# A two-layer decoder in one kernel: another order of heads, transposes and jobs in the top-k indexer, and a shorter selection

## The reference

```
logits = einsum('bqhd,bkd->bqhk', qi, k_idx) * (IDX_DIM ** -0.5)       # 8 heads of 64
score  = einsum('bqhk,bqh->bqk', relu(logits), wi * (IDX_HEADS ** -0.5))
score  = where(causal, score, -inf)
_, idx = top_k(score, 256)          # the 256 best keys of a query; ties go to the lower index
```

## Time and profile before

| | |
|---|---|
| median of three runs | 1347.61 us (1347.42 to 1348.81) |
| the profiled execution, its own time | 1348.37 us |
| its span (first to last instruction) | 1346.5 us |
| TensorE busy | 1302.9 us, 97% |
| VectorE busy | 803.5 us, 60% |
| ScalarE busy | 563.1 us, 42% |
| GpSimd busy | 524.6 us, 39% |
| granted TensorE clock, mean | 0.99 |

### The profile page before, as it was taken

How to read it: one execution, slowest core, us unless ns; L and a number is a source line. 1 busy time by engine, 2 the same in 40 slices (tenths; PEclk the granted TensorE clock), 3 DMA queues, 4 the chain that set the end, 5 groups by cost and what they waited for, 6 DMA issues and landing times. The chain is left out here.

```text
span 1346.5 us, 19019 instructions
## 1 busy us (share of the span) xinstructions
PE 1302.9 (97%) x6890; PEld 1111.5 (83%) x6890; DVE 803.5 (60%) x1581; ACT 563.1 (42%) x1134; POOL 524.6 (39%) x721
## 2 busy tenths in 40 slices
PE   9999999999999999999987999999899999999997
PEld 8878888989898888888766788888788988888885
DVE  7624755555556345245577889977977776345233
ACT  8312244554454023123235665564266666023122
POOL 2842034554443744234401132331066564744201
PEclk9999999999999999999998999999999999999999
DMA  6232331121101522133300122342222221521122
GB/s 203 77 106 78 112 116 56 55 71 48 55 32 56 175 87 75 60 96 120 95 0 1 55 87 89 110 140 67 88 72 64 79 63 64 153 95 59 60 65 87
DMA packets 83372, 110.07 MB, mean 82 GB/s; under 512 B 9552, under 2 KB 45648, under 8 KB 83280
## 3 DMA queue, kind: packets, MB, share of 16 engines
q1 hardware_dynamic: 83280, 108.86, 26.0%
HBM read 81.04 MB, written 27.79 MB: 81 GB/s over the span
## 5 line engine op out<-in xcount | busy, mean ns | idle before, releaser
L1700 PE MATMUL psum<-ring_hi,act_lo 128*128 128x512 f32 x816 | 322.4, 395 | 0.7 <-DVE act_lo L1688 0.7
L1702 PE MATMUL psum<-ring_hi,act_hi 128*128 128x512 f32 x816 | 318.9, 391 | 0.0
L1701 PE MATMUL psum<-ring_lo,act_hi 128*128 128x512 f32 x816 | 318.8, 391 | 0.0
L1126 POOL CAST ring_hi<-raw 128x512 fp32r<-128x512 f32 x128 | 81.8, 639 | 322.6 <-DMA raw<-in_dsa_w_in 144.0
L1341 DVE TENSOR_TENSOR act_lo<-psum,act_hi 128x512 fp32r<-128x512 f32 (+3 forms) x276 | 156.0, 594 | 67.2 <-ACT act_hi L1170 40.9
L1129 POOL TENSOR_TENSOR ring_lo<-raw,ring_hi 128x512 fp32r<-128x512 f32 x128 | 180.0, 1406 | 10.4
L1700 PEld LDWEIGHTS psum<-ring_hi,act_lo 128*128 128x128 f32 x816 | 154.1, 189 | 32.8 <-DVE act_lo L1688 1.4
L1702 PEld LDWEIGHTS psum<-ring_hi,act_hi 128*128 128x128 f32 x816 | 153.8, 188 | 32.3
L1701 PEld LDWEIGHTS psum<-ring_lo,act_hi 128*128 128x128 f32 x816 | 154.1, 189 | 31.0
L1170 ACT ACTIVATE act_hi<-psum 128x512 fp32r<-128x512 f32 (+1 forms) x244 | 114.9, 511 | 150.2 <-PE psum L1912 80.5
L1140 POOL TENSOR_TENSOR small<-small 128x1 f32<-128x1 f32 x128 | 70.7, 552 | 228.7 <-ACT p L1308 169.8
(11 more groups left out here) (257 smaller groups left out, 2473.7 us busy)
## 6 DMA issues: line engine op xcount, KB each, us to landing
raw<-in_dsa_w_in SPq DMA_DIRECT2D x48, 256.0 KB, 3.1
gz<-z_scratch SPq DMA_DIRECT2D x16, 512.0 KB, 3.6
raw<-in_ple_w_gate SPq DMA_DIRECT2D x32, 256.0 KB, 3.1
raw<-in_mla_w_in SPq DMA_DIRECT2D x19, 256.0 KB, 2.9
xr<-in_x_t SPq DMA_DIRECT2D x16, 256.0 KB, 6.8
z_scratch<-gz SPq DMA_DIRECT2D x16, 256.0 KB, 2.0
raw<-in_mla_w_out SPq DMA_DIRECT2D x16, 256.0 KB, 3.4
p<-in_x SPq DMA_DIRECT2D x16, 256.0 KB, 3.1
```

What stands on the lines that cost most here:

```text
L1126: last = nc.gpsimd.tensor_copy(dst, src[:, c0:c0 + cols])
L1700: nc.tensor.matmul(dst, lhs(1), rhs(0), start=start, stop=False)
L1701: nc.tensor.matmul(dst, lhs(0), rhs(1), start=False, stop=False)
L1702: return nc.tensor.matmul(dst, lhs(0), rhs(0), start=False, stop=stop)
```

## The change

In the indexer, heads are single steps (one bank or one pair each) instead of pairs, and all jobs from the first head on (heads, transposes, projections) take ring A and ring B in turn (`next_ring`). The order within tile t becomes: heads 0 to 3 of t, transposes of t+1, query job of t+2, heads 4 to 7. In tiles 6 and 7, which have no further query job, a key/value job stands there (`KV_EARLY = 2`), so six are left behind the indexer. The third query job is issued before the heads of tile 2. The rotated query rows go to two slots at the end of `xr` instead of `p1`, and there is a third ReLU row slot behind the scores. The weights of the key/value chunk are issued ahead of the heads, not one piece per query job.

In the search ScalarE counts tiles 5, 6, 7 (before 3, 6, 7), VectorE 2, 3, 4. There are still 32 rounds; gate jobs 2 and 5 carry two, since two key/value jobs no longer carry one. `last_step` counts only ScalarE's tiles and sets the threshold; `above` is gone. In `sel`, ScalarE makes a row of signs with its sum in `xr` behind the scores, and VectorE has an equality pass, a running count with a start value, a small step for the limit, and one last pass. The tiles are selected in the order 6, 4, 7, 3, 5, 2.

```diff
-SEARCH = [2, 4, 5, 3, 6, 7]
-ACT_TILES = [3, 6, 7]
+SEARCH = [2, 3, 4, 5, 6, 7]
+ACT_TILES = [5, 6, 7]
+KV_EARLY = 2
+TWO_ROUNDS = (2, 5)
+SELECT = [6, 4, 7, 3, 5, 2]
...
+    kv_weights(0, 1)
+    qi_job(FULL)
+    kv_weights(2, 3)
     fk.append(key_job(1, 0, 1).after["fk"])
     rots = [key_back(1, job, fk[job]).after["rot"] for job in range(2)]
-    qi_ready = {FULL: qi_split(FULL, rot[FULL])}
-    rot[FULL + 1] = qi_job(FULL + 1)
+    qi_split(FULL)
+    kv_weights(4)
+    qi_job(FULL + 1)
+    kv_weights(5)
     for job in range(2):
         lo_at["kiT"] = key_split(1, job, rots[job])
-    for t in range(FULL, T):
+    qi_job(FULL + 2)
+    kv_weights(6, 7)
+    idx_scores(FULL, range(4))
+    qi_split(FULL + 1, next_ring())
+    idx_scores(FULL, range(4, IDX_HEADS))
+    add("idx_mask", None, t=FULL)
+    for t in range(FULL + 1, T):
+        idx_scores(t, range(4))
         if t + 1 < T:
-            qi_ready[t + 1] = qi_split(t + 1, rot[t + 1])
+            qi_split(t + 1, next_ring())
         if t + 2 < T:
-            rot[t + 2] = qi_job(t + 2)
-        idx_scores(t, qi_ready[t])
+            qi_job(t + 2, next_ring())
+        elif t - T + 2 < KV_EARLY:
+            kv_job(t - T + 2, next_ring())
+        idx_scores(t, range(4, IDX_HEADS))
+        add("idx_mask", None, t=t)
...
+    for t in range(KV_EARLY, T):
+        for job in range(KV_EARLY) if t == KV_EARLY else ():
+            ahead(next_chunk(1, 2), job)
+        ahead(next_chunk(1, 2), t)
+        kv_job(t)
+        search()
...
-    after_bits = [("last_step", None, {}), ("above", None, {})]
-    after_bits += [("sel", {"found": 1}, {"t": t}) for t in range(FULL, T)]
+    after_bits = [("last_step", {"thr": 1}, {})]
+    after_bits += [("sel", {"found": 1, "sgn": 1}, {"t": t, "side_free": max(0, j - 1)}) for j, t in enumerate(SELECT)]

     def z_extra(k):
         search()
+        if k in TWO_ROUNDS:
+            search()
...
+        relu_rows = [gz[:], t2[:], xr[:, SCORE_AT[T]:SCORE_AT[T] + S]]
...
             if n > CW:
-                return (gz, t2)[k % 2][:, 0:n]
-            return (gz, t2)[k // 2 % 2][:, k % 2 * CW:k % 2 * CW + n]
+                return relu_rows[k % 3][:, 0:n]
+            return relu_rows[k // 2 % 3][:, k % 2 * CW:k % 2 * CW + n]
...
+                    k = s.before["sc"]
+                    act_e.wait_ge(sem["b_full"], s.after["b_full"])
+                    if n["keys"] > CW:
+                        act_e.wait_ge(sem["sc"], max(k - 2, 2 * IDX_HEADS))
+                    elif k >= 6:
+                        act_e.wait_ge(sem["sc"], k - 5)
+                    elif k == 0:
+                        act_e.wait_ge(sem[n["gfree"][0]], n["gfree"][1])
+                    elif k == 4:
+                        act_e.wait_ge(sem["x2_st"], n["x2"])
...
                             dve.wait_ge(sem["cs_ld"], n["cs"])
-                            dve.wait_ge(sem["hi"], s.before["hi"])
+                            dve.wait_ge(sem["x2_st"], n["x2"])
+                            if n["stack_read"]:
+                                dve.wait_ge(sem["hi"], n["stack_read"])
...
-                    for i, t in enumerate(SEARCH):
+                    linked(nc.vector.memset(cnt[:, 0:SPREAD - len(ACT_TILES)], 0.0))
+                    for t in ACT_TILES:
+                        i = SEARCH.index(t)
...
                     linked(nc.vector.tensor_scalar(eq, score_at(t), thr, None, ALU.is_equal))
-                    linked(nc.vector.tensor_tensor_scan(order, eq, eq, 0.0, ALU.add, ALU.max))
-                    linked(nc.vector.scalar_tensor_tensor(eq, order, need[:, i:i + 1], eq, ALU.is_le, ALU.mult))
-                    nc.vector.scalar_tensor_tensor(score_at(t), score_at(t), thr, eq, ALU.is_gt,
-                                                   ALU.add).then_inc(sem["found"], 1)
+                    linked(nc.vector.tensor_tensor_scan(order, eq, eq, float(2 * keys - 4 * TOPK), ALU.add, ALU.add))
+                    dve.wait_ge(sem["sgn"], s.after["sgn"])
+                    linked(nc.vector.scalar_tensor_tensor(need[:, i:i + 1], order[:, keys - 1:keys], 0.5, cnt[:, i:i + 1],
+                                                          ALU.mult, ALU.add))
+                    nc.vector.scalar_tensor_tensor(score_at(t), order, need[:, i:i + 1], side_at(t), ALU.is_le,
+                                                   ALU.is_gt).then_inc(sem["found"], 1)
```

More of the change, by code:

```diff
@@ L606, in plan @@
     last_rows = tail(0, 4, "in1", ("lo", now["lo"]))
-    def idx_scores(t, q_ready):
-        keys = (t + 1) * P
[L611 to L617, removed]
@@ L618, in plan, with next_ring, idx_scores @@
-    idx_n = [0]
+    turn = [0]
+    def next_ring():
+        turn[0] += 1
+        return "BA"[turn[0] % 2]
+    def idx_scores(t, heads):
+        keys = (t + 1) * P
+        for h in heads:
+            add("idx", {"b_full": 1, "relu": 1, "sc": 1}, ring=next_ring(), jobs=1, freed=["relu"],
+                wide=keys > CW, t=t, h=h, keys=keys, q_ready=max(qi_ready[t], lo_at["kiT"]),
+                x2=now["x2_st"], gfree=read_by["G"])
     fk = [key_job(1, 0, 0).after["fk"]]
     norm_b(last_rows[0], 0, last_rows[1])
-    def qi_job(t):
-        w(next_chunk(1, 1), t)
-        return rope_job(1, 1, t, t % 2, cs=cs.after["cs_ld"]).after["rot"]
@@ L626, in qi_split, with qi_job @@
[L626 to L631, removed]
+    rot, qi_ready, stack_read = {}, {}, {}
+    def qi_job(t, ring="A"):
+        rot[t] = rope_job(1, 1, t, t % 2, cs=cs.after["cs_ld"], stack_read=stack_read.get(t - 2), ring=ring,
+                          x2=now["x2_st"]).after["rot"]
@@ new lines, in qi_split, with kv_job, kv_weights @@
+    def qi_split(t, ring="B"):
+        s = add("qi_split", {"b_full": 2, "hi": 2, "lo": 2}, ring=ring, jobs=2, freed=["lo"], slot=t % 2, rot=rot[t])
+        stack_read[t] = s.after["hi"]
+        qi_ready[t] = s.after["lo"]
+    def kv_job(t, ring="A"):
+        slot = t % 2
+        rope_job(1, 2, t, slot, extra_inc={"st%d" % slot: 1, "vcopy": 1}, st_before=now["st%d" % slot], ring=ring)
+    def kv_weights(*rows):
+        for d in rows:
+            w(next_chunk(1, 1), d)
+    kv_weights(0, 1)
@@ L663, in search @@
         search_end(search_begin())
-    n = 0
-    for i, name in ((2, "kv"), (3, "q"), (4, "q")):
+    for t in range(KV_EARLY, T):
[4 more added lines that the diff above has]
+        search()
+    for i in (3, 4):
         for t in range(T):
             ahead(next_chunk(1, i), t)
[L669 to L679, removed]
+            slot = t % 2
+            st = search_begin()
+            rope_job(1, i, t, slot, extra_inc={"st%d" % slot: 1}, base=(i - 3) * CW, st_before=now["st%d" % slot])
+            search_end(st)
     q_stored = (now["st0"], now["st1"])
@@ L1295, in _ @@
                 elif k == "idx":
[L1296 to L1304, removed]
+                    k = s.before["sc"]
[8 more added lines that the diff above has]
+                        act_e.wait_ge(sem["x2_st"], n["x2"])
+                    nc.scalar.activation(relu_slot(k, n["keys"]), bank(s.banks[0], n["keys"]), ACT.Relu,
+                                         scale=IDX_SCALE).then_inc(sem["relu"], 1)
                 elif k == "E":
@@ L1548, in _ @@
                     dve.wait_ge(sem["widx"], s.before["widx"])
[L1549 to L1558, removed]
-                            nc.vector.tensor_scalar(dst, src, wcol, None, ALU.mult).then_inc(sem["sc"], 1)
-                        else:
-                            nc.vector.scalar_tensor_tensor(dst, src, wcol, dst, ALU.mult, ALU.add).then_inc(sem["sc"], 1)
+                    h, k = n["h"], s.before["sc"]
+                    dve.wait_ge(sem["relu"], s.after["relu"])
+                    if k == 0:
+                        dve.wait_ge(sem["x2_st"], n["x2"])
+                    else:
+                        dve.wait_ge(sem["sc"], k)
+                    src = relu_slot(k, n["keys"])
+                    wcol = wis[:, t * IDX_HEADS + h:t * IDX_HEADS + h + 1]
+                    if h == 0:
+                        nc.vector.tensor_scalar(dst, src, wcol, None, ALU.mult).then_inc(sem["sc"], 1)
+                    else:
+                        nc.vector.scalar_tensor_tensor(dst, src, wcol, dst, ALU.mult, ALU.add).then_inc(sem["sc"], 1)
                 elif k == "idx_mask":
@@ L1759, in _ @@
                             c = (4 * j + i) * P
-                            last = nc.tensor.transpose(bank(s.banks[j])[:, i * P:(i + 1) * P], p1[:, c:c + P], ident[:])
+                            last = nc.tensor.transpose(bank(s.banks[j])[:, i * P:(i + 1) * P],
+                                                       qi_stack(n["slot"])[:, c:c + P], ident[:])
                         last.then_inc(sem["b_full"], 1)
```

41 lines of the change are left out of this document (23 added, 18 removed).

## The result

The changed kernel takes **1332.75 us** (median of 4 runs, 1332.07 to 1333.47) against 1347.51 us for the kernel before on the same chip: a ratio of 0.9892, 95% interval 0.9876 to 0.9907, some 14.8 us faster. A second set, on another chip, gave 1333.64 against 1347.34 us, 0.9898 (0.9885 to 0.9912). The forecast was 1331.2 us in a range of 1325.5 to 1339.5. The profiled execution took 1332.53 us.

The account below looks back on a forecast made before the run. TensorE, busy nearly all of 1346.5 us, bounds the kernel; only the indexer and the border can give. 1348.37 less 16.4 (indexer 16.2, border 0.2) is 1332.0, less 0.76 to the median: 1331.2 us; range 1325.5 to 1339.5.

Parts of the forecast that it names:

- two common points: Indexer: from the end of the keys' transposes (665.33 us) to the end of last head and two key/value jobs.
- the large ones: Indexer: TensorE pauses of 3.4 us before tile 3's later heads and 2.4 us before tile 5's transposes.
- Low clock twice: Indexer: after each of the two large pauses TensorE runs at its low clock level, losing 1.4 us each time.
- my 67.6: Indexer: TensorE's work in us between the two points, from transposes 4.0, jobs 32.7 and heads 30.9.
- The new order, step by step: Indexer: walk through the new order of heads, transposes and jobs; last head ends at 743.2, 16.2 us off TensorE's path.
- rival (a): Indexer: only the last tiles gain, pauses of tiles 3 to 5 return; 8.8 us, 1338.8 us; chance 12%.
- Rival (d): Indexer: TensorE's clock stays low with more waits, so slower; 1388 us if from tile 3 on; chance 5%.
- this half at 0.2 us: Search and selection: the attention starts 0.2 us earlier at the border; below that 0, above 2.0.
- some 3: Search: gate jobs 2 and 5 with two rounds leave a lag of some 3 us at slot 7, no gain or loss.
- over 10 us: Selection: VectorE's chain behind slot 7 ends over 10 us before the z jobs do.
- my 29: Selection: us left of VectorE's 42.0 us chain behind slot 7 after the change takes out counts and passes.
- The edits at nothing: Moved key/value stores, weight loads, POOL's splits and the new wait for saved rows: priced at nothing.

Follow-up runs that it names:

- experiment 5: experiment 2's kernel with the kernel before's banks (heads on rings A, A, B, B, transposes on B, jobs on A): 1338.74 us, ratio 0.9938.
- experiment 8: Changed kernel with all eight heads after the transposes and both key/value jobs behind the last head: 1337.46 us, ratio 0.9929.
- experiment 2: Changed kernel with the old order inside a tile (transposes, job, then eight heads): 1330.84 us, on another chip 1330.28 us.
- experiment 7: Changed kernel with the wide ReLU rows shifted by one, so the first is not the last narrow rows' memory: 1330.41 us, ratio 0.9876.
- experiment 10: Changed kernel with the edits of experiment 6 and experiment 7 together: 1327.38 us, ratio 0.9862.
- experiment 1: Changed kernel with both key/value jobs back behind the indexer and no gate job with two rounds: 1340.32 us, ratio 0.9947.
- experiment 6: Changed kernel with the third query job, then tile 3's transposes, ahead of tile 2's eight heads; old order from tile 3: 1326.91 us, ratio 0.9847.
- experiment 9: Kernel before with only the new search split and selection: 1347.19 us against 1347.11 us, ratio 0.9999.
- experiment 4: Changed kernel with the kernel before's search split, last step, 'above' and selection: 1335.1 us, ratio 0.9907.

## Why the prediction was right, and where it was not

**The place and the size.** It read that only the stretch from 671 to 748 us had anything to give, and measured both kernels between two common points: 16.2 us forecast, 15.65 measured. The job behind the last head was put at 743.2 and came at 743.75, the attention's gain at 16.4 and came at 16.1. The forecast is 1.5 us off the first set, and two sets of the one kernel are 0.9 apart.

**The pauses, one by one.** Forecast at 677.7, 694.1, 704.5 and 717.1; found at 677.76, 694.88, 704.34 and 717.32, the first three with the releasers named. The fourth is put down to a ReLU of ScalarE, which ended 0.15 us behind the rotation (717.33 against 717.18), and a fifth, of 0.49 us at 690.77, was not forecast. Forecast 3.4 and 2.4 us for the large ones, found 1.87 each: with 0.99 at 673.85 the first sum is 2.86, since the transposes waited too, and I had not counted that wait. Together the pauses were forecast at 7.2 us (3.4 + 2.4 + 1.4) and measured at 7.0. Low clock twice, at 1.4 us each, was forecast; in the profiled execution it came once and cost 1.7 (granted clock 0.57 from 679 to 683 us). The 1.4 came from dividing the low clock of the kernel before into four stretches; its trace from 671 us on has three (0.76 over 700 to 707 us, 0.72 over 717 to 723, 0.62 over 728.5 to 733) and the tail of one. By these terms the last head should have ended 1.3 us earlier than forecast. It did not, since TensorE's work between the points was counted too low: 665.29 to 743.75 less 7.0 and 1.7 leaves 69.8 us for my 67.6. From one start to the next, less the pauses, the heads took 32.85 us (counted 30.9), the six jobs 33.6 (32.7) and the transposes 5.0 (4.0), the 1.7 of low clock included. Two errors of 1.3 and 2.2 us partly cancel, so that 743.2 is so near to 743.75 is partly luck.

**The cause was put in the wrong place.** The step that failed is "The new order, step by step", in what it credits: the order as such. It followed the new program rightly for the most part, but a right walk through the new order does not say which of its edits a pause owes its end to. By the runs: banks in turn 8.5 us (experiment 5 kept the single heads, whose own worth was not tried), early key/value jobs 6.6 to 7.6, third row up to 1, the order inside a tile -1.9 to -3.4. The prediction saw the bank: its first paragraph says that the pair on ring A wants the query job's bank. But it put the wait down to the order of the tile, and gave the banks in turn no price; "single heads release banks sooner" is a remark under rival (a). The two halves also stand without each other: banks in turn without early jobs are 9.7 us below the kernel before (experiment 8), early jobs with the old banks 8.6 (experiment 5). Their sum is 1.2 to 1.9 us more than the two together gave (experiment 2: 16.3 and 17.1). If the parts add up, that is what both runs hold in common: single heads, the third row, the slots of the query rows. This is an estimate from these runs, and no run takes the single heads out. What the new order costs is in good part one ReLU row: with the rows shifted (experiment 7) the changed order comes to 1330.41 us, level with the old order's 1330.28 and 1330.84. In the best order the shift is worth nothing (experiment 10).

**Rival (a), the last tiles alone.** Forecast 8.8 us for the order and the jobs of the last tiles. The jobs alone gave 7.6, so the rival had a true part, but the first tiles gained as much again: the transposes of tile 7 begin at 721.39, where they began at 728.51 before. My expectation of experiment 1 had only 4 us: it left out the wait for tile 7's low half.

**Rival (d) did not come.** The clock was 0.98 over the heads, and 1.00 in experiments 2, 6 and 7, with four or five waits of 0.5 to 2.0 us in each. The Trainium skill (TensorE: Matmul & The Clock Gate, section "A second HAM failure mode: psum-queue depth-cycling") tells of brief idling that lowers the clock. In these traces waits of up to 1.2 us never did, as in the earlier trace rows; pauses of 1.86 to 1.97 us did so in some executions and not in others (last section), and never long enough for (d).

**The search and the selection.** I cost this half at 0.2 us; alone it is worth between -0.9 and 1.3 us by its interval (experiment 9), inside the changed kernel 1.5 to 2.4 or, by the rows, at least 1.3 (experiment 4). The lag that I forecast for the two slots with two rounds, "some 3", explains it, and came at 2.6. The last round ends 6.1 us after its job now (913.9 against 951.38 - 43.6 = 907.8), 3.5 in the kernel before (927.0 against 923.5, the transposes there starting at 967.07), and 3.8 in experiment 1, which has no such slot (919.8 against 959.56 - 43.6). In experiment 4, with the slots of two rounds and the old split over the engines, the last round ends at 912.5, 4.5 us after its job, and the old last step, counts and selection take 41.8 us from there, as in the kernel before (927.0 to 968.9). They end at 954.35, where the transposes begin at 951.63, and TensorE waits. Beside the 3.5 of the kernel before, the two slots add 1.0 us with the old split, the new split adds 0.3 without them (experiment 1), and both together add 2.6. The new selection is short enough for that. The margin was smaller than "over 10 us", though. VectorE's last steps (L1690 waits for ScalarE's Sign, L1289):

```profile
936.66 0.16 DVE L1690 SCALAR_TENSOR_TENSOR small<-cs,small 128x1 f32<-128x1 f32 x1 [1.15 <-ACT xr L1289]
...
942.32 0.16 DVE L1690 SCALAR_TENSOR_TENSOR small<-cs,small 128x1 f32<-128x1 f32 x1 [2.26 <-ACT xr L1289]
...
947.44 0.16 DVE L1690 SCALAR_TENSOR_TENSOR small<-cs,small 128x1 f32<-128x1 f32 x1 [2.58 <-ACT xr L1289]
947.63 0.62 DVE L1692 SCALAR_TENSOR_TENSOR xr<-cs,small,xr 128x384 f32<-128x384 f32 x1
952.70 1.29 DVE L1393 TENSOR_TENSOR act_lo<-psum,act_hi 128x512 fp32r<-128x512 f32 x2 [4.45 <-ACT act_hi L1210]
```

It ends at 948.25, 3.1 us before the z jobs: each Sign stands behind a Silu in ScalarE's queue, which comes once per z job, and the 6.0 us of waits were not in my 29. They cost nothing, as the 4.45 us of idle time behind them show.

**The edits at nothing.** The moved stores and weight loads and the new wait for the saved rows show no wait of TensorE: between 655 and 760 us none is put down to a DMA or to GpSimd, and from 743 to 952 us TensorE is busy throughout. No table load stands between 905 and 954 us, where six Signs alternate with Silus.

## What to carry to other kernels

When several edits are made at once, price each one against the waits that it alone could end, banks and buffers as well as the order: here a job's pending bank, not the place of the job, stopped TensorE. Handing banks out in turn over everything that runs, instead of by kind of work, was worth 8.5 us here, and independent work from the next stage, put where the other engine was catching up, 6.6 to 7.6. An edit that is worth nothing alone, as the selection here, can pay for the delay that another one brings.

## What the runs showed of the hardware that was not expected

The low clock after a pause of about 1.9 us is not certain. Before the transposes of tile 3, 1.97 us of pause brought it in the kernel before (669.69 and 670.12 in the earlier trace rows, 0.43 apart); in experiment 2, 1.96 us at the same place and time did not (669.00 and 669.23, 0.23 apart). In the changed kernel one pause of 1.87 us was followed by it (679.29 and 679.72) and the next, of 1.87, was not. In experiment 5 one of 2.45 us was (0.75 from 702 to 706 us) and one of 2.24 us was not (1.00 from 715 to 719). The two pauses of over 3 us in experiments 1 and 8, at 731.32 and 723.68, both were, and no wait of 1.2 us or less was. As one such stretch costs 1.6 to 1.7 us (the query job behind the second 1.87 us pause took 5.54 us in the changed kernel's first profiled execution and 7.17 in the second), a sum over a few pauses carries an uncertainty of that size, and the two executions differ so: their last head ended at 743.75 and at 744.92 with the same waits, at a clock of 0.98 and 0.95 from 671 to 743 us.
